# A hybrid S5 and stick-breaking decoder step on one core: layout changes moved from TensorE transposes to transfers

## The reference, cut to what matters

```python
def s5_scan(u, h0, A_re, A_im, log_dt, B_re, B_im, C_re, C_im, D):
    uf = u.astype(f32).reshape(b, L, SSM_GROUPS, SSM_GROUP_SIZE)
    lam = lax.complex(A_re, A_im)
    dt = jnp.exp(log_dt)[:, None]
    a_bar = jnp.exp(lam * dt)
    b_bar = ((a_bar - 1.0) / lam)[:, :, None] * lax.complex(B_re, B_im)
    bu = jnp.einsum('blgc,gpc->blgp', uf, b_bar)
    bu = bu.at[:, 0].add(a_bar[None] * h0)
    ...  # h[t] = a_bar * h[t-1] + bu[t], by an associative scan
    y = jnp.real(jnp.einsum('blgp,gcp->blgc', h, c)) + D * uf
    return y.reshape(b, L, SSM_WIDTH), h[:, -1]
```

## Time and profile before

| | |
|---|---|
| median of 3 runs | 3087.73 us (3087.71 to 3088.34) |
| the profiled execution | 3084.51 us, span 3082.4 us |
| granted PE clock, mean | 0.994 |
| PE busy | 3012.3 us (98% of the span) |
| DVE, ACT, POOL busy | 1357.4, 1037.2, 466.6 us |
| DMA, mean | 101 GB/s |

### The profile page before, as it was taken

One profiled execution on the slowest core, in us unless ns is written; L12 is line 12 of the kernel. 1 busy time (PEld: TensorE's weight loads), 2 busy tenths in 40 slices (PEclk: granted clock), 3 DMA queues, 4 the chain that ended last, 5 costly groups with the idle time before them and its releaser, 6 DMA issues.

```text
span 3082.4 us, 49205 instructions
## 1 busy us (share of the span) xinstructions
PE 3012.3 (98%) x19516; PEld 2939.6 (95%) x19516; DVE 1357.4 (44%) x2564; ACT 1037.2 (34%) x1330; POOL 466.6 (15%) x1126
## 2 busy tenths in 40 slices
PE   5999999999999999999999999999999999999997
PEld 5999999999999999999999999999999999999997
DVE  6624443462444345244434524443465444422266
ACT  6135315413521441352154136215421321212242
POOL 6400330050033015003301400330013000000000
PEclk8999999999999999999999999999999999999999
DMA  6131223223222322222232231222439654342283
GB/s 177 50 107 58 73 68 97 71 58 97 68 65 66 97 71 64 91 69 69 63 95 72 65 97 63 76 67 85 139 123 301 218 190 158 93 133 68 81 240 110
DMA packets 400899, 312.41 MB, mean 101 GB/s; under 512 B 58339, under 2 KB 365107, under 8 KB 398643
## 3 DMA queue, kind: packets, MB, share of 16 engines
q1 hardware_dynamic: 400690, 309.44, 33.2%
HBM read 227.30 MB, written 65.27 MB: 95 GB/s over the span
## 4 chain that ended last, share of the span: by engine, by line
PE 90%; DVE 4%; ACT 2%; issue 2%; DMA 1%; SPq 0%; POOL 0%; DVEq 0%; POOLq 0%; ACTq 0%
PE acc L1765 80%; PE side L1730 4%; PE side L1933 2%; PE side L1928 1%; DVE work L1499 1%; DMA work<-in_cache_v 1%; ACT w_high L856 0%; PE side L1864 0%; PE side L1863 0%; PE side L1875 0%; PE side L2049 0%; DMA work<-in_x_prompt 0%; DVE work L1506 0%; DVE work L1500 0%; DVE x_low L1359 0%
## 5 line engine op out<-in xcount | busy, mean ns | idle before, releaser
L1765 PE MATMUL acc<-x_high,w_high 128*128 128x344 f32 (+2 forms) x5440 | 1224.4, 328 | 18.2 <-ACT w_high L856 5.3
L1765 PE MATMUL acc<-x_low,w_high 128*128 128x344 f32 (+2 forms) x5440 | 1181.5, 320 | 0.0
L1765 PE MATMUL acc<-x_high,w_low 128*128 128x344 f32 (+2 forms) x5440 | 1177.4, 320 | 0.0
L1765 PEld LDWEIGHTS acc<-x_high,w_high 128*128 128x128 f32 x5440 | 906.9, 189 | 39.8 <-issue 17.4
L1765 PEld LDWEIGHTS acc<-x_low,w_high 128*128 128x128 f32 x5440 | 921.9, 189 | 0.0
L1765 PEld LDWEIGHTS acc<-x_high,w_low 128*128 128x128 f32 x5440 | 913.1, 188 | 0.0
L856 ACT CAST w_high<-w_raw 128x1024 fp32r<-128x1024 f32 x232 | 242.3, 1044 | 891.5 <-PE acc L1765 827.7
L1344 DVE TENSOR_TENSOR w_low<-w_raw,w_high 128x1024 fp32r<-128x1024 f32 x233 | 290.3, 1246 | 551.2 <-ACT w_high L856 548.5
L1215 POOL COPY work<-s_tables 128x28 f32 x16 | 3.3, 206 | 1548.6 <-DMA work<-t_state_seeds 1390.0
L1492 DVE TENSOR_TENSOR work<-work,side 128x128 f32<-128x128 f32 x64 | 18.4, 287 | 317.4 <-PE side L1933 317.4
L1730 PE MATMUL side<-work 128*128 128x128 f32 (+5 forms) x704 | 136.2, 311 | 0.0
(11 more groups left out here) (315 smaller groups left out, 2529.7 us busy)
## 6 DMA issues: line engine op xcount, KB each, us to landing
w_raw<-in_w_in SPq DMA_DIRECT2D x160, 512.0 KB, 3.9
w_raw<-in_w_out SPq DMA_DIRECT2D x48, 512.0 KB, 4.0
work<-t_sig_ga SPq DMA_DIRECT2D x24, 516.0 KB, 4.7
out<-work SPq DMA_DIRECT2D x18, 512.0 KB
t_qk<-stage SPq DMA_DIRECT2D x16, 516.0 KB, 5.1
work<-t_qk SPq DMA_DIRECT2D x16, 516.0 KB, 4.5
t_sig_gb<-stage SPq DMA_DIRECT2D x16, 516.0 KB, 4.2
t_sig_ga<-stage SPq DMA_DIRECT2D x16, 516.0 KB, 4.2
```

The source lines that it names most:

```text
L1765: ins = mm(acc[s][:, a, 0:n], w[b][:, kk, :], x[:, kx, c0:c0 + n], start=start, stop=stop)
```

## The change

u is stored to DRAM (`t_u`, with the columns ordered by offset) and read back by eight transfers into `Ug`, and by a ninth into `Us`; y is stored by eight transfers a half (`t_y_by_offset`) and read back by one into `yT`. For that the two operands of the matmuls for y change sides, so that y comes out with offset and channel as rows. The twenty-four large transposes of a pass (`XJ`, `UG`, `YT`) and the eight small products of `US` are gone, and so are ACT's copies between them. The four transposes of the states become one of 32 rows, and their store becomes eight transfers in place of two. DVE's doublings stand in two pieces, five at `TURN` and two four steps later. `KM` of the first half moves from step 11 to 12. The last step of y is at 40 in place of 38. The sixteen products with the identity at the end (L2091) become transposes.

```diff
+            def u_groups():
+                sp.wait_ge(u_ready, i + 1)
+                sp.dma_start(t_u, uT).then_inc(u_sent, 16)
+                sp.dma_start(t_us.unsqueeze(2), u_off[:, :, NCH:NCH + 1], allow_slow_non_contiguous=True).then_inc(u_sent, 16)
+                sp.wait_ge(u_sent, (i + 1) * 32)
+                rows = t_u.rearrange("(g c) (t j) -> t c g j", c=GC, t=CH)
+                for tau in range(CH):
+                    sp.dma_start(Ug[tau * GC:(tau + 1) * GC], rows[CH - 1 - tau][:, :, 0:NCH]).then_inc(ug_in, 16)
+                sp.dma_start(Us, t_us.rearrange("(g c) b -> c g b", c=GC)).then_inc(ug_in, 16)
+            def y_rows(hf):
+                sp.wait_ge(yj_ready, i * 2 + hf + 1)
+                rows = t_yj.rearrange("(g c) (t j) -> t c g j", c=GC, t=CH)
+                for t in range(CH):
+                    sp.dma_start(rows[t][:, hf * HG:(hf + 1) * HG],
+                                 xy[t * GC:(t + 1) * GC, hf * 512:(hf + 1) * 512].rearrange("p (g j) -> p g j", g=HG)).then_inc(yj_sent, 16)
+            def y_back():
+                sp.wait_ge(yj_sent, (i + 1) * 256)
+                sp.dma_start(yT, t_yj).then_inc(yj_in, 16)
                 for part, out in ((0, re_sample), (1, im_sample)):
-                    sp.dma_start(out[0, :, bass.ds(g0, HG), :], SO[:, :, part * 64:(part + 1) * 64]).then_inc(st_sent, 16)
+                    for g in range(HG):
+                        sp.dma_start(out[0, :, bass.ds(g0 + g, 1), :].rearrange("b a n -> b (a n)"),
+                                     SO[g * NEW:(g + 1) * NEW, part * 64:(part + 1) * 64]).then_inc(st_sent, 16)
+                if cn == 2:
+                    u_groups()
                 if cn == 6:
+                    y_rows(0)
                     s5_states(0)
                     s5_seeds(1)
                 if cn == 10:
+                    y_rows(1)
+                    y_back()
                     s5_states(1)
-    ... KM ... = ... (11, 27) ...
-    XJ, UG, US, YT = 9, 10, 12, 38
+    ... KM ... = ... (12, 27) ...
+    YN, YT = 38, 40
-                nc.scalar.copy(tok3(uT), acc_v(0)).then_inc(u_ready, 1)
+                nc.scalar.copy(uT.rearrange("p (t b j) -> p b j t", t=CH, b=NB), acc_v(0).rearrange("p b (j t) -> p b j t", t=CH)).then_inc(u_ready, 1)
...
-                        for g in range(HG):
-                            dst = xy[:, 0:SEQ].rearrange("p (t f) -> p t f", t=CH)[:, :, hf * 64 + g * GC:hf * 64 + (g + 1) * GC]
-                            last_op = nc.scalar.copy(dst, side[:, 0, g * P:(g + 1) * P].rearrange("p (t c) -> p t c", t=CH))
-                        last_op.then_inc(yj_ready, 1)
+                        nc.scalar.copy(xy[:, hf * 512:(hf + 1) * 512], side[:, 0, :]).then_inc(yj_ready, 1)
-                        nc.scalar.copy(SO, side[0:NEW, 0, :].rearrange("p (g s) -> p g s", g=HG)).then_inc(ys_ready, 1)
+                        nc.scalar.copy(SO, side[0:HG * NEW, 0, 0:P]).then_inc(ys_ready, 1)
...
-                        turning(i, hf, ch)
+                        turning(i, hf, ch, range(5))
+                    if p == TURN[hf] + 4:
+                        turning(i, hf, ch, range(5, 7))
...
+                    dve.wait_ge(yj_in, i * 16 + 16)
+                    V.scalar_tensor_tensor(xy[:, 0:SEQ].rearrange("p (j t) -> p t j", t=CH), u_off[:, :, 0:NCH], dcol[:, bass.ds(i, 1)],
+                                           y_off, ALU.mult, ALU.add).then_inc(yt_ready, 1)
...
-                            mm(out, Ug[:, HG * hf + g, :], Toep[:, g, :], start=True, stop=False)
-                            mm(out, V1[:, g, 0:NCH], N1[:, g, GC:9 * GC], start=False, stop=True)
+                            mm(out, Toep[:, g, :], Ug[:, HG * hf + g, :], start=True, stop=False)
+                            mm(out, N1[:, g, GC:9 * GC], V1[:, g, 0:NCH], start=False, stop=True)
...
-                            last_op = tr(side[0:NEW, 0, g * P:(g + 1) * P], hn[:, g, :], ident[:, :])
-                        last_op.then_inc(ys_mm, 1)
+                        tr(side[0:HG * NEW, 0, 0:P], hn_flat, ident[:, :]).then_inc(ys_mm, 1)
```

More of the change, by code:

```diff
@@ L148, in build @@
     t_qs = dram("t_q_new", [NEW, WIDTH])
+    t_u, t_us, t_yj = dram("t_u", [P, TOK]), dram("t_u_new", [P, NEW]), dram("t_y_by_offset", [P, SEQ])
     t_n, t_h = dram("t_output_seeds", [2, P, WIDTH]), dram("t_state_seeds", [2, P, GROUPS * NEW])
@@ L183, in build @@
     uT, xy = c.take(TOK), c.take(TOK)
-    Ug = c.take(8 * NCH).rearrange("p (g j) -> p g j", g=8)
+    yT = c.take(8 * NCH)
+    Ug = yT.rearrange("p (g j) -> p g j", g=8)
+    u_off, y_off = uT.rearrange("p (t j) -> p t j", t=CH), yT.rearrange("p (t j) -> p t j", t=CH)
     m_flat = c.take(1024)
@@ L201, in build @@
     PT = [v_flat[:, 256 * n:256 * n + 256] for n in range(4)]
-    SO = c.take(HG * P, NEW).rearrange("p (g s) -> p g s", g=HG)
+    SO = c.take(P, HG * NEW)
     Bc, Bm = c.take(HG * GC), c.take(HG * GC)
@@ L207, in build @@
     hA = c.take(HG * NEW).rearrange("p (g b) -> p g b", g=HG)
-    hn = c.take(HG * NEW).rearrange("p (g b) -> p g b", g=HG)
+    hn_flat = c.take(HG * NEW)
+    hn = hn_flat.rearrange("p (g b) -> p g b", g=HG)
     ysT = c.take(P, NEW)
@@ L286, in build @@
         ("s5_b_mm", "s5_bt_ready", "s5_k_mm", "s5_kt_ready", "s5_kt_pad", "s5_toep_in")]
[L287 to L288 removed]
+    u_sent, ug_in, yj_sent, yj_in, pq_mm, v_ready, y_mm, yj_ready, fin_ready, p_copied, t_ready, swap_in = [sem(s) for s in
+        ("s5_u_sent", "s5_ug_in", "s5_yj_sent", "s5_yj_in", "s5_pq_mm", "s5_v_ready", "s5_y_mm",
          "s5_yj_ready", "s5_fin_ready", "s5_p_copied", "s5_scanned", "s5_swapped_in")]
@@ L1405, in y_low, with turning @@
             V.tensor_tensor(XL[:, t, :], f32(XL[:, t, :]), f32(XH[:, t, :]), ALU.subtract).then_inc(xb_ready, 1)
-        def turning(i, hf, ch):
-            ch(V.tensor_copy(turn[:, 0:3, :], tab[:, 4:7, bass.ds(i * (2 * HG) + hf * HG, HG)]),
-               V.memset(Er[:, :, 0:1], 1.0), V.memset(Ei[:, :, 0:1], 0.0))
+        def turning(i, hf, ch, powers):
+            if 0 in powers:
+                ch(V.tensor_copy(turn[:, 0:3, :], tab[:, 4:7, bass.ds(i * (2 * HG) + hf * HG, HG)]),
+                   V.memset(Er[:, :, 0:1], 1.0), V.memset(Ei[:, :, 0:1], 0.0))
             er, ei, sq, both = turn[:, 0, :], turn[:, 1, :], turn[:, 3:5, :], turn[:, 5, :]
-            for k in range(7):
+            for k in powers:
                 w = 1 << k
@@ L2090, in _ @@
         for f in range(KT):
-            last = one(acc[f // 8][0:NEW, 1 + f // 4 % 2, f % 4 * P:(f % 4 + 1) * P], outs_new[:, f, :], ident[:, :])
+            last = tr(acc[f // 8][0:NEW, 1 + f // 4 % 2, f % 4 * P:(f % 4 + 1) * P], outs_new[:, f, :], ident[:, :])
         last.then_inc(osm_tr, 1)
```

77 lines of the change are left out of this document (17 added, 60 removed).

## The result

The changed kernel takes 3098.2 us (median of 5 runs, 3092.9 to 3100.3) beside 3087.7 for the kernel before on the same chip (5 runs, 3081.3 to 3088.3): ratio 1.0039, 95% interval [1.0026, 1.0051]. It is slower by 8 to 16 us, where I had forecast 4.5 us faster. The profiled execution, the fastest of the five, took 3092.89 us, span 3090.8, mean granted clock 0.988 (0.994 before).

The account below looks back on a forecast made before the run. PE, busy 3012.3 of 3082.4 us, was taken to bound the kernel. 40.0 us gained less waits of 10.4, 20.8 and 4.3 gave 4.5 faster, 3083.2 us from 3087.73; range 3063 to 3104.

Parts of the forecast that it names:

- the sum: 40.0 us gained on PE less 35.5 us lost to waits: net 4.5 faster, 3083.2 us counted from 3087.73.
- POOL, the swaps and the weight loads keep their places: Claim that these stay where they were in the schedule; no cost was given to them.
- wrong altogether if PE waits at `PQ`: The forecast's own sign of failure in the changed kernel's profile: any wait of PE at `PQ`, given no price.
- PE's work: Gain on PE: 36.2 us over eight passes, 1.9 at the end, 1.9 from a first-pass wait; 40.0 in all.
- The wait for the low half of chunk 3: First pass: PE waited 1.86 us behind seven doublings on DVE; with two moved behind that split, it goes.
- Wait one: PE at `YM` of the first half, for DVE's rotation: mean 1.3 us a pass, 10.4 in eight.
- Wait two: PE at `KM` of the second half, for POOL's output weights after late seeds: 2.6 us a pass, 20.8 in eight.
- Wait three: Turn of v: PE at `VT` waits for loads issued after y's store, 0.7 us in six passes, 4.3 in all.
- The u path: u through DRAM from step 8 takes 12.7 us, `PQ` comes some 18 later; single words hidden in the margin of 5.
- rival 4: The u path takes over 18 us, each microsecond over costing 8 us; with 2 over, 3099 us; chance 0.05.
- Rival 1: Stores of y issue as cheaply as those of states (0.33 us); Wait two falls to 3.2: 3065.6 us; chance 0.20.
- rival 2: y through DRAM: small stores land in 4.5 us, not 2.0; PE waits 24.6 at v's turn: 3103.5 us; chance 0.24.

Follow-up runs that it names:

- e2: Changed kernel with 24 unread transposes on PE where it would wait at `KM` of the second half: 3081.7 us, ratio 0.9990.
- e9: Kernel before with 21 idle stores ahead of the second half's seeds, plus 40 unread transposes on PE in place of the wait: 3121.7 us, ratio 1.0118.
- e7: Changed kernel with second-half seeds first, single words on their own semaphore and `KM` of the first half at step 11: 3046.5 us, ratio 0.9879.
- e12: Kernel before with only the states' part of the change, one transpose and eight stores: 3071.8 us, ratio 0.9964.
- e1: Changed kernel with the second half's seed loads issued ahead of the stores of y and states at chunk 6: 3068.6 us, ratio 0.9942.
- e10: Changed kernel with only `KM` of the first half moved back to step 11: 3091.2 us, ratio 1.0023.
- e13: Changed kernel with only `KM` moved, to steps 11 and 28 in place of 12 and 27: 3065.6 us, ratio 0.9940.
- e3: Changed kernel with the store of single words `t_u_new` on its own semaphore and `Us` waited for at `YM`: 3087.2 us, ratio 1.0016.
- e6: Changed kernel with second-half seeds issued first and the single words on their own semaphore: 3062.5 us, ratio 0.9926.
- e5: Kernel before with 21 idle stores issued ahead of the second half's seeds at chunk 6: 3136.2 us, ratio 1.0167.
- e8: Kernel before with 12 idle stores issued ahead of the second half's seeds at chunk 6: 3097.6 us, ratio 1.0039.
- e11: Changed kernel with seeds first, single words on their own semaphore, `KM` at 11 and rotation tables in one piece again: 3050.0 us, ratio 0.9885.

## Why the prediction was wrong

**The step that failed** is the sum: a wait was priced at its length. "Behind it on PE stand all matmuls of the next steps, so nothing hides it" was true and not enough, since those matmuls then run at half clock. The term is missing altogether; by the stretches it is 17.0 us in the profiled execution (nine of them, an estimate), and e2 and e9 show it by taking it away without taking away what made PE wait. With it my own sum is 3083.2 + 17.0 = 3100.2, and the runs' median 3098.2. The sum comes so close because other errors in it cancel, as below.

A second step failed without moving the sum much: "POOL, the swaps and the weight loads keep their places". They didn't: the state seeds landed 1.5 us later against PE, and POOL's work took longer beside the doublings in two pieces. And by my own sign ("wrong altogether if PE waits at `PQ`") I was wrong: it waited there, in two passes.

Point by point:

- **PE's work, 40.0 less.** A little low. e7, which has all of the work removed, is 38.6 us below the kernel before beside it, and still has 5.7 us of new waits. From one `KM` of the second half to the next, PE's waits taken out, a pass takes 267.1 us before and 262.1 in e7 (within 0.1 in six of seven passes of either): 5.0 less, where I had 4.52. The states have the most of it, 1.5 a pass by e12 where I had 1.26. The products at the end gave 1.75 (3.66 to 1.91 us), as forecast. The wait for the low half of chunk 3, 1.9 us, was to go; it is 0.35 in the profiled execution of the changed kernel and 0.3 to 3.2 in the seven others with the tables in two pieces.
- **Wait one, 10.4.** Measured 6.5, seven times of about 0.9. The cause was as argued, the step that `KM` was given: e7 takes it away but for one wait of 2.0. Missing: the same lateness reaches POOL's second half through SP's list.
- **Wait two, 20.8.** Measured 22.5, 2.73 in the third pass against 2.6. That is right for a cause that is right in part. The stores of y cost 0.49 each (3.88 / 8) where I took 0.60, and eight stores of states 3.17 where I took 2.64 (8 x 0.33). But e1, with the seeds in front, keeps 10.0 us of the wait. In its third pass the slack of 2.6 us goes to POOL's later start (4.94 - 3.27 = 1.7), its longer work (26.06 in place of 24.68, 1.4) and to PE's way from `YM` to `KM`, 29.8 us in place of 30.5 (0.7): 1.2 us over, and PE waits 1.23.
- **Wait three, 4.3.** Measured none. `VT` and ACT's wait ahead of it, which answer to the earlier trace rows:

```profile
751.80 1.03 PE L1899 MATMUL side<-ident,work 128*128 128x128 f32 x8
```

```profile
750.44 1.03 ACT L875 ACTIVATE work<-acc 128x1032 f32<-128x1032 f32 x1 [1.77 <-DMA work<-stage]
```

  The slack is 1.36, as before. y's store is late as forecast, 4.8 us behind the split of chunk 11 (740.83 after 736.04) where it had been 2.5. But I carried that through to the loads one to one. Before, SP issued the loads of attention 4.19 us behind the store of y, the first two in 2.12 us; now it is 2.67 and 0.82:

```profile
733.89 0.36 SPq L488 DMA_DIRECT2D t_y<-work  x1
738.08 2.12 SPq L497 DMA_DIRECT2D work<-t_qk  x2
```

```profile
740.83 0.36 SPq L519 DMA_DIRECT2D t_y<-work  x1
743.50 0.82 SPq L528 DMA_DIRECT2D work<-t_qk  x2
```

  So y reached the loads 2.8 us sooner than I carried it. The median landing of y's store is the greater part: 4.2 us from its issue before, 2.7 now. The other part is the issue of the first two loads, 1.3 us less. Before, that store was issued 1.1 us behind the load of a weight chunk (732.78), now 3.4 (737.43); whether that is the reason was not tested.
- **The u path, at no price.** Wrong by 5.1 us of waiting and two stretches of half clock. The store of 1024 single words landed after 7.9 to 12.6 us, median 8.8, and the loads stand behind it. With the words as changed this wait is there twice in the changed kernel, once in e1, e10 and e13 (2.5 to 2.6 us), and 0.3 us in e2; with the words apart (e3, e6, e7) it is never over 0.4. In the first pass:

```profile
85.80 0.61 SPq L474 DMA_DIRECT2D t_u_new<-work  x1
98.38 1.77 SPq L478 DMA_DIRECT2D work<-t_u  x4
...
102.09 0.43 SPq L479 DMA_DIRECT2D work<-t_u_new  x1
```

  I had priced the words by nothing at all and called them hidden; rival 4 named the path, and gave it 0.05.
- **The rivals.** None was what happened. Rival 1 is out by 0.49 for a store of y, rival 2 by their landing, 1.8 us in the median; rival 4 named the path of the waits at `PQ`, but they are 5.1 us in two passes and not each pass. Two of the forecast's three waits were there; the time came out toward the upper end of the range (3104) for a reason that was no case of mine. That a wait could change the pace of what follows belonged among the rivals, with the question of e5 and e8: how long may PE stand still?

## What to carry to other kernels

Price a wait of the bounding matrix engine by its length only while it is short: here 1.4 us cost about 1.4, and behind 39 of 44 waits of 2.5 us and more the matmuls ran at 1.2 GHz for a while, at a price of some 1.7 us or more. By these numbers two short waits are better than one long one (no run splits one), and a kernel that takes work from PE must pay its new lateness in pieces or move the step that waits. Before moving transfers ahead of others in one queue, ask who waits for the one pushed back (two seeds behind eighteen stores), and before moving a step later, follow what it delays through every engine's list: the late rotation held back `YM`, and in SP's list the state seeds that POOL needed. The same change with the seeds in front, the single words on their own semaphore and `KM` where it had been (e7) is 1.2% faster than the kernel before, ratio 0.9879 [0.9864, 0.9894].

## What the runs showed of the hardware that I had not expected

- The clock behind a wait goes by its length, but not sharply. All waits of PE of 0.8 us and more between 80 and 2190 us of the fourteen traces of this case, and how many had a stretch at 0.50 within the next 6 us:

| wait, us | waits | half clock behind |
|---|---|---|
| 0.8 to 1.7 | 152 | 0 |
| 1.7 to 2.5 | 17 | 8 |
| 2.5 to 3.6 | 31 | 26 |
| 3.6 to 6.8 | 13 | 13 |

  A stretch is of 3.4 us, in some cases 6.8. Waits of the same 2.71 us, at 962 and at 1230 in the changed kernel, went one each way; what decides between them isn't settled. It may be what makes runs of one program differ: e10, with waits around 2.9 us, spread over 14.6 us.
- A store of 128 x 8 single words took 8.8 us to land, when a store of 516 KB in rows took 3.0 in the same kernel.
- `scalar_tensor_tensor` over 128 x 1024 with two strided sides took 2.25 us on DVE, 1.22 in the contiguous form of the earlier trace rows.
- The same instructions on POOL took longer by what DVE did meanwhile: with the doublings in two pieces its second half took 1.1 us more up to the end of the output weights than with one (e7 and e11, 25.7 and 24.6 us in seven and six of their eight passes). The output weights by themselves took 10.75 us before, 11.4 in the changed kernel and 12.0 in e1. Which of DVE's instructions does it is not shown.
